# Expert weight slots released by halves, with the down projection loaded, multiplied, split and scattered by column halves

## The reference

```
expert_id, gate = top-1 group, top-2 experts of that group      # per token
y[e] = (silu(xb @ w_gate[e]) * (xb @ w_up[e])) @ w_down[e]      # w_gate, w_up: 1024 x 512, w_down: 512 x 1024
x = x + sum over the token's two experts of gate * y[e][token]
```

## Time and profile before

| | before |
|---|---|
| median of three runs | 2009.35 us |
| the profiled execution, its own time | 2013.8 us |
| its span, first to last instruction | 2011.9 us |
| TensorE matmul busy | 1909.7 us, 95% |
| VectorE, ScalarE, GpSimd busy | 29%, 19%, 8% |
| bytes moved by DMA | 476.99 MB, 237 GB/s on average |
| granted TensorE clock | 0.98 |

### The profile page before, as it was taken

The page is one execution under the profiler, slowest core; times in us unless marked ns, Lnnn a source line. Parts: engine busy times, 40 slices in busy tenths (PEclk is TensorE's granted clock), DMA queues, the critical chain, the costliest instruction groups (busy, mean ns, idle before and its releaser), DMA issues.

```text
span 2011.9 us, 18702 instructions
## 1 busy us (share of the span) xinstructions
PE 1909.7 (95%) x7688; PEld 938.4 (47%) x7688; DVE 579.4 (29%) x1089; ACT 374.1 (19%) x627; POOL 157.0 (8%) x144
## 2 busy tenths in 40 slices
PE   5999999898999999999889999998979999999997
PEld 4445644534444454444343444444444544445443
DVE  2799210223122222222212312103232222222222
ACT  2333311212111111111023322111121101111013
POOL 0466210001000000000020000200100000000001
PEclk9999999998999999999999999998989999999998
DMA  9115422202899999999951211220049999999994
GB/s 356 44 47 177 156 84 84 84 0 84 304 393 394 395 392 396 391 396 393 394 208 42 84 42 42 96 87 30 0 171 395 392 396 391 395 393 394 394 392 173
DMA packets 204462, 476.99 MB, mean 237 GB/s; under 512 B 7614, under 2 KB 8044, under 8 KB 203980
## 3 DMA queue, kind: packets, MB, share of 16 engines
q1 hardware_dynamic: 203260, 470.88, 62.8%
q0 software_dynamic: 496, 2.53, 0.4%
q10 hardware_dynamic: 608, 2.24, 0.3%
HBM read 471.43 MB, written 4.19 MB: 236 GB/s over the span
## 4 chain that ended last, share of the span: by engine, by line
PE 66%; SPq 19%; DVE 8%; ACT 2%; DMA 2%; issue 2%; ACTq 0%; DVEq 0%
SPq L915 19%; PE PS L422 17%; PE PS L556 13%; PE PS L378 13%; PE PS L570 7%; DVE PS L1639 5%; PE PS L608 4%; PE PS L593 4%; PE PS L846 3%; DMA ring<-in_moe_w_up 1%; PE PS L429 1%; PE PS L582 1%; ACT hT L1091 1%; PE PS L503 1%; DMA R<-in_conv_w_dw 1%
## 5 line engine op out<-in xcount | busy, mean ns | idle before, releaser
L422 PE MATMUL PS<-hT,ring 128*128 128x512 f32 x640 | 279.2, 598 | 6.9 <-ACT hT L1065 6.0
L556 PE MATMUL PS<-ring,xg 128*64 128x512 f32 x1024 | 228.8, 596 | 10.7 <-DMA ring<-in_moe_w_up 6.4
L556 PE MATMUL PS<-ring,hT 128*64 128x512 f32 x1024 | 227.2, 595 | 2.5 <-DMA ring<-in_moe_w_up 2.1
L570 PE MATMUL PS<-ring,hT 128*64 128x512 f32 x1024 | 226.8, 595 | 2.7 <-ACT hT L1152 2.7
L1528 DVE TENSOR_TENSOR xT<-PS,xT 128x512 f32<-128x512 f32 x256 | 158.5, 681 | 223.2 <-PE PS L593 223.2
L422 PEld LDWEIGHTS PS<-hT,ring 128*128 128x128 f32 x640 | 122.2, 192 | 159.5 <-issue 158.7
L556 PEld LDWEIGHTS PS<-ring,xg 128*64 128x64 f32 x1024 | 71.9, 137 | 145.7 <-issue 145.3
L556 PEld LDWEIGHTS PS<-ring,hT 128*64 128x64 f32 x1024 | 72.9, 137 | 135.8 <-issue 135.1
L570 PEld LDWEIGHTS PS<-ring,hT 128*64 128x64 f32 x1024 | 70.7, 137 | 135.3 <-issue 127.6
L1011 POOL TENSOR_TENSOR dg<-memT 128x512 f32<-128x512 f32 x6 | 7.6, 1270 | 1556.5 <-ACT memT L1060 1556.5
L1554 DVE TENSOR_TENSOR ylo<-PS,yhi 128x1024 fp32r<-128x1024 f32 x32 | 39.2, 1224 | 300.3 <-ACT yhi L1157 300.3
(11 more groups left out here) (249 smaller groups left out, 1780.8 us busy)
## 6 DMA issues: line engine op xcount, KB each, us to landing
ring<-in_moe_w_gate SPq DMA_DIRECT2D x128, 1024.0 KB, 16.1
ring<-in_moe_w_up SPq DMA_DIRECT2D x128, 1024.0 KB, 14.4
ring<-in_moe_w_down SPq DMA_DIRECT2D x128, 1024.0 KB, 14.6
ring<-in_xa_w_kv SPq DMA_DIRECT2D x16, 1024.0 KB, 7.3
ring<-in_gla_w_in SPq DMA_DIRECT2D x12, 1024.0 KB, 14.7
ring<-in_conv_w_in SPq DMA_DIRECT2D x8, 1024.0 KB, 14.8
ring<-in_xa_w_q SPq DMA_DIRECT2D x8, 1024.0 KB, 6.9
ring<-in_xa_w_o SPq DMA_DIRECT2D x8, 1024.0 KB, 6.9
```

The lines of the kernel that those rows point to most:

```text
L422: mm = pe.matmul(bank(b), w[:, k * 512 + m * P:k * 512 + (m + 1) * P], src[:, k, :], start=(k == 0), stop=(k == C - 1))
L556: mm = pe.matmul(PS[e * SL:(e + 1) * SL, kind * BANK:(kind + 1) * BANK], x[:, k, (2 * (p % 2) + e) * SL:(2 * (p % 2) + e + 1) * SL], ring[ ...
L570: mm = pe.matmul(PS[e * SL:(e + 1) * SL, (2 + half) * BANK:(3 + half) * BANK], hidT[:, k, e * SL:(e + 1) * SL], ring[:, pair_slot(l, 4 + e ...
```

## The change

1. **Release by halves.** In `up` the semaphore is incremented twice, after the matmuls of rows 0 to 511 and after those of 512 to 1023. `pair_loads` waits for each half before it issues that half of both experts. All waits on these semaphores count twice as far.
2. **Down by column halves.** A half of a down slot now holds columns 0 to 511 or 512 to 1023 of all 512 rows. `down` runs over the column half outermost: 16 matmuls for bank 2, an increment of `y_full`, 16 matmuls for bank 3, another increment.
3. **The result by halves.** `yhi` and `ylo` are made in two instructions each of 128 x 512, each after its half; `scatter` waits for the first half of `ylo` before its first chunk and for the second half before chunk 4.

```
-                    mm.then_inc(g[key], 1)
+                        if k % 4 == 3:
+                            mm.then_inc(g[key], 1)
 
                 def down(p):
                     pe.wait_ge(g["hidT_ready"], NP * r + p + 1)
-                    for k in range(FC):
-                        if k % 2 == 0:
-                            for e in range(2):
-                                loaded(p, 4 + e, k // 2)
-                        for half in range(2):
+                    for half in range(2):
+                        for e in range(2):
+                            loaded(p, 4 + e, half)
+                        for k in range(FC):
                             for e in range(2):
                                 mm = pe.matmul(PS[e * SL:(e + 1) * SL, (2 + half) * BANK:(3 + half) * BANK],
                                                hidT[:, k, e * SL:(e + 1) * SL],
-                                               ring[:, pair_slot(l, 4 + e), k * D + half * 512:k * D + (half + 1) * 512],
+                                               dst_half(pair_slot(l, 4 + e), half)[:, k * 512:(k + 1) * 512],
                                                start=(k == 0), stop=(k == FC - 1))
-                    mm.then_inc(g["y_full"], 1)
+                        mm.then_inc(g["y_full"], 1)
...
                 def scatter(p, cs):
+                    pe.wait_ge(g["ylo_done"], 2 * (NP * r + p - 1) + 1)
                     if cs[0] == 0:
-                        pe.wait_ge(g["ylo_done"], NP * r + p)
                         taken(p - 1, 11)
                     for c in cs:
+                        if c == 4:
+                            pe.wait_ge(g["ylo_done"], 2 * (NP * r + p))
                         b, done = use(p, 1 + c)
...
                 for kind, key in enumerate(("gate_full", "up_full", "y_full")):
-                    for e in range(2):
-                        if p or not isinstance(r, int):
-                            sp.wait_ge(g[key], NP * r + p)
-                        elif first_wait is not None:
+                    if first_wait is not None and not p:
+                        for e in range(2):
                             sp.wait_ge(*first_wait[2 * kind + e])
                     for h in range(2):
+                        if p or first_wait is None:
+                            sp.wait_ge(g[key], 2 * (NP * r + p - 1) + 1 + h)
                         for e in range(2):
-                            j = 2 * kind + e
-                            slot = pair_slot(l, j)
-                            nk = C if kind < 2 else FC
+                            slot = pair_slot(l, 2 * kind + e)
                             w = a[("moe_w_gate", "moe_w_up", "moe_w_down")[kind]][l, 2 * p + e]
-                            w = w.rearrange("(k p) n -> p k n", p=P)[:, h * nk // 2:(h + 1) * nk // 2, :]
-                            sp.dma_start(dst_half(slot, h).rearrange("p (k n) -> p k n", k=nk // 2),
-                                         w).then_inc(ld[slot][h], 16)
+                            w = w.rearrange("(k p) n -> p k n", p=P)
+                            w = w[:, h * 4:(h + 1) * 4, :] if kind < 2 else w[:, :, h * 512:(h + 1) * 512]
+                            sp.dma_start(dst_half(slot, h).rearrange("p (k n) -> p k n", k=4), w).then_inc(ld[slot][h], 16)
...
-                    act.wait_ge(g["y_full"], NP * r + p + 1)
-                    act.activation(yhi[:, :], PS[:, 2 * BANK:4 * BANK], ACT.Copy).then_inc(g["yhi_done"], 1)
+                    for half in range(2):
+                        act.wait_ge(g["y_full"], 2 * (NP * r + p) + 1 + half)
+                        act.activation(yhi[:, half * 512:(half + 1) * 512], bank(2 + half), ACT.Copy).then_inc(g["yhi_done"], 1)
...
-                    dve.wait_ge(g["yhi_done"], NP * r + p + 1)
-                    dve.tensor_tensor(ylo[:, :], PS[:, 2 * BANK:4 * BANK], yhi[:, :].bitcast(F32),
-                                      ALU.subtract).then_inc(g["ylo_done"], 1)
+                    for half in range(2):
+                        cols = slice(half * 512, (half + 1) * 512)
+                        dve.wait_ge(g["yhi_done"], 2 * (NP * r + p) + 1 + half)
+                        dve.tensor_tensor(ylo[:, cols], bank(2 + half), yhi[:, cols].bitcast(F32),
+                                          ALU.subtract).then_inc(g["ylo_done"], 1)
```

More of the change, by code:

```diff
@@ L925, in _ @@
                         j = n - RING - moe_base[l - 1] - RING * (NP - 1)
-                        sp.wait_ge(seg[l - 1][("gate_full", "up_full", "y_full")[j // 2]], NP)
+                        sp.wait_ge(seg[l - 1][("gate_full", "up_full", "y_full")[j // 2]], 2 * NP)
                     for h in range(2):
@@ L944, in _ @@
                     for key in ("gate_full", "up_full", "y_full"):
-                        sp.wait_ge(seg[l][key], NP * ROUNDS)
+                        sp.wait_ge(seg[l][key], 2 * NP * ROUNDS)
             o_dram = out.rearrange("b (t p) d -> (b t) p d", p=P)
@@ L1147, in moe_segment @@
                     more = q + 1 < NQ
-                    act.wait_ge(g["gate_full"], NP * r + p + 1)
+                    act.wait_ge(g["gate_full"], 2 * (NP * r + p + 1))
                     act.wait_ge(g["gates_ready"], NP * r + p + 1)
@@ L1547, in moe_segment @@
                     dve.wait_ge(g["silu_done"], NP * r + p + 1)
-                    dve.wait_ge(g["up_full"], NP * r + p + 1)
+                    dve.wait_ge(g["up_full"], 2 * (NP * r + p + 1))
                     dve.scalar_tensor_tensor(hidden, sil, gcol, bank(1), ALU.mult,
```

## The result

The changed kernel takes 2014.3 us, the median of 20 runs, against 2009.85 for 20 runs of the kernel before: ratio 1.0023, 95% interval 1.0014 to 1.0032. In a second series beside other kernels it was 1.0030 (1.0015 to 1.0045). It is slower, by 4.5 us where 6.9 were forecast, inside the range. One of the 20 runs took 2246.43 us at a granted clock of 0.841 and is left out of the ratio.

A forecast was written before the change was run, and what follows sets the result against it. The weight transfer stream was taken as the bound. Per layer 8.0 - 3.5 - 1.05 = 3.45 us longer, 6.9 for both, on the median of 2009.35 gives 2016.2 us (0.34% slower); its own range 2012 to 2021, the wider range 2006 to 2024.

The forecast's parts named there:

- The bound: Expert parts: transfers need 31.9 us a pair against TensorE's 31.2, so the weight stream sets each layer's end.
- Part 1: Start of each layer's expert stream: release by halves issues the first load of pair 1 3.5 us earlier, kept throughout.
- Part 2: Down loads: 2048-byte pieces cost 0.56 us more per pair, making each layer 8.0 us later.
- The rate of 387: Down loads: GB/s expected with 2048-byte pieces, in place of 408 with 4096.
- 14.3 downs: Down loads ahead of the last up load in each layer's stream, each costing 0.56 us more.
- The bound from `gla_w_in`: Down loads: that load's 382 GB/s as the worst rate, a price of 0.70 us a pair, 10.0 a layer.
- One small step: Down on TensorE: the same 32 matmuls in column-half order were to take 7.0 us again.
- Part 3: End of each layer: splitting the result by halves brings the first scatter matmul 1.05 us closer to the last down.
- The sum: Whole program: 8.0 - 3.5 - 1.05 = 3.45 us longer per layer, 6.9 for both.
- The chances: Whole program: 0.57 for slower, 0.31 for within 0.3%, 0.12 for faster.

The follow-up runs named there:

- e8: Kernel before with gate and up in 8192-byte pieces released by halves, down in 4096-byte pieces released whole, result by halves: 1987.19 us, ratio 0.9874.
- e1: Kernel before with only the release by halves added, down still in 4096-byte pieces and the result split whole: 2003.91 us, ratio 0.9970.
- e2: Kernel before with only the column halves of down added, slots released whole and the result split whole: 2020.91 us, ratio 1.0068.
- e11: The changed kernel run again unaltered, for a second profile, against the kernel before: 2014.54 us, ratio 1.0030.
- e9: The changed kernel with gate and up loaded in 8192-byte pieces, feature order permuted once a layer: 1985.88 us, ratio 0.9875 to the kernel before.
- e3: The changed kernel with only the split of the result undone, made whole again: 2016.83 us, ratio 1.0044 to the kernel before.
- e6: Kernel before with all expert loads in 1024-byte pieces, strided weight loads, gate and up released by halves, result by halves: 2141.87 us, ratio 1.0667.
- e7: Kernel before with all expert loads in 2048-byte pieces, strided weight loads, gate and up released by halves, result by halves: 2111.54 us, ratio 1.0536.

## Why the prediction was right

**The bound.** Right. The stream sets the end of each expert part while gate and up come in short pieces; e8 shows what TensorE needs by itself, 8 us a layer less.

**Part 1, 3.5 us earlier.** 3.52 us in the issue (508.68), 3.6 and 3.8 at the end in e1. No gap opened: from 520 to 540 us the rate of the changed kernel is 387 throughout.

**Part 2, 8.0 us later.** 7.9 and 8.4 in e2. The rate of 387 and the count of 14.3 downs both held. The bound from `gla_w_in` (382) was a reading of one stretch: in the 5 us before it that load runs at 386, and in the same window at 387 in e2 and 388 in the changed kernel.

One small step was wrong: the last `down` was to take 7.0 us again. In column halves it takes 7.31 and 7.18 us in the two layers against 7.11 and 7.09 before, since its second half starts 3.66 us after the first (999.57 and 1003.23) and not 3.5. The wait rows do not say what it waited for.

**Part 3, 1.05 us.** 2.35 against 1.33 us, 1.0, and by the steps that were forecast: `yhi` of the second half (1006.92, 0.60 us), the copy of `onehotT` (1007.51, 0.60), and the scatter at 1008.21, while the second `ylo` ends at 1008.24. With the longer `down` 0.8 and 1.0 are left.

**The sum.** From the first gate matmul to the first scatter matmul after the last pair a layer takes 503.2 and 503.0 us where it took 499.3 in both, so 3.9 and 3.75 us more where 3.45 stood: 7.7 for both, and 7.8 in e11. The program as a whole became only 4.5 us longer (2.8 to 6.4 by the interval). The step that was off is the silent one, that the rest stays as it is. The profiles show how little that holds. From the start of layer 0's last `down` to layer 1's first gate matmul the profiles count 1360 or 1361 matmuls in every kernel. That stretch before, in the changed kernel, and in e9:

```profile
994.86:1488.24 493.38, 463.85 (x1361) 221.23 (x1361) 116.41 (x276) 111.68 (x208) 31.50 (x28) 0.96 0.23 82
```

```profile
999.57:1487.00 487.43, 458.82 (x1360) 219.67 (x1361) 116.61 (x277) 111.82 (x209) 31.50 (x28) 0.97 0.23 84
```

```profile
984.59:1468.84 484.25, 455.67 (x1360) 218.06 (x1361) 116.55 (x277) 111.83 (x209) 31.51 (x28) 0.98 0.20 75
```

The last column but two is the granted clock: 0.96, 0.97 and 0.98, and TensorE is busy for 463.9, 458.8 and 455.7 us with the same work. The stretch takes 493.4, 487.4 and 484.3 us, of which the shorter tail explains 0.8. In the attention, where TensorE waits for the other engines now and then, the clock falls from 2.4 to 1.2 GHz for short times. Eight matmuls of one form in the kernel before, first after a wait of 2.95 us and then 13 us later, take 6.62 and 3.67 us:

```profile
1359.45 6.62 PE L378 MATMUL PS<-hT,RK 128*128 128x512 f32 x8 [2.95 <-ACT hT L1052]
...
1372.76 3.67 PE L378 MATMUL PS<-hT,RK 128*128 128x512 f32 x8 [2.36 <-ACT hT L1052]
```

In some executions this happens more often than in others. The 40 us from 1360 (not quite the same work in the two kernels) have a mean clock of 0.85 before and 1.00 in the changed kernel:

```profile
1360.00:1400.00 40.00, 32.17 (x94) 17.91 (x93) 13.92 (x31) 7.93 (x22) 0.00 (x0) 0.85 0.05 18
```

```profile
1360.00:1400.00 40.00, 29.09 (x101) 16.87 (x101) 14.32 (x33) 10.75 (x32) 0.00 (x0) 1.00 0.14 53
```

So 5.1 of the 7.7 us were given back there in the first profile of the changed kernel and 2.9 of 7.8 in the second (489.6 us). e1 took 493.5 for this stretch, e2 488.5.

The other executions show how much of the total goes with the clock, since each has its mean granted clock on record. Those of e11 and of the kernel before beside it, at the clocks that both have:

| mean granted clock | 0.982 | 0.984 | 0.986 |
|---|---|---|---|
| before, mean us (executions) | 2011.7 (2) | 2006.8 (3) | 2003.7 (2) |
| changed, mean us (executions) | 2017.3 (2) | 2013.9 (4) | 2010.3 (2) |

At the same clock the changed kernel is 5.6, 7.1 and 6.6 us slower; over all 31 executions of it and 63 of the kernel before that have a clock on record, it is 6.0 to 7.4, near the 7.7 of the profiles. The medians differ by less, and the clocks differ too: 0.9838 on average for the changed kernel, 0.9825 before. Whether the change itself makes the clock fall less often stays open; e3, whose expert parts are as long, averages 0.9822 over 12.

**The chances.** 0.57 stood on slower by over 0.3%, 0.31 on within. The result, 0.23%, is within, so the larger chance stood on the wrong side of the line; the second series (0.30%) lies on it. The forecast of 0.34% was close to the line, and so is the difference at an equal clock, 0.28 to 0.37%. The interval of the first leaves out 1.000 all the same: a small loss, and a real one.

## What to carry to other kernels

When a transfer stream and an engine both look full, compare their periods and look for what the engine waits for late in the stage; then price an edit by the stream's rate, and read that rate per kind of load, not as one mean. Giving buffers back in finer pieces moves such a stream once, by the time of one piece at its start; anything that lowers its rate is paid on every byte, so do not buy the first with the second. Choose which rows a partition takes so that each piece is long: here that alone, made free by permuting the other operand once, was worth 0.9%. With the finer halves beside it 1.25% was measured; the shorter tail explains 0.1 of the difference, and those executions also had the higher clock.

## What the runs showed of the hardware

- A piece of a transfer from DRAM costs about 8.8 ns beside its bytes on each of 16 engines: 348, 387, 408 and 419 GB/s at 1024, 2048, 4096 and 8192 bytes. The Trainium skill, page "DMA: Bandwidth & Descriptors", section "Why small descriptors are slow (HBM only)", has a cost of the same form, about 3 cycles per packet, and about half the size: 2.3% between 2048 and 4096 bytes is an estimate from its figures, 5.4% were measured here. Its section "Specifications" asks for 512 bytes only, and e6 lost 10% of the rate at twice that against 2048.
- Column halves of 2048 bytes, cut out of rows of 4096, run at the same 387 GB/s as rows of 2048 bytes read whole, and as the pieces of 2048 bytes of e7 (388), which lie one behind the other.
- A TensorE weight load of 128 x 128 float32 whose columns lie 32 bytes apart took 336 ns, against 195 for neighbouring columns; writes by ScalarE and VectorE in the permuted order took no longer than before (597 and 690 ns).
- The same 1360 or 1361 matmuls between the two expert parts took 484 to 494 us over the ten profiles in which they were compared, with the granted clock between 0.98 and 0.96. In a kernel of 2000 us that is more than the whole effect of this change.
- Executions of the kernel before took 2004.2 us on average at a mean granted clock of 0.986 (9 of them) and 2013.0 us at 0.980 (17).
